# A hybrid decoder step: S5 recurrence as scans, stacked sample products, four state buffers

## The chip, the cores and the metric

The program runs on one core of a Trainium2 chip. The metric is the device time of one execution in microseconds (us), as the median of several runs. PE is the tensor engine, DVE the vector engine, ACT the scalar engine, POOL the GpSimd engine and SP the queue that issues most loads.

## The reference

One step of a two-layer trunk over a prompt of 256 tokens and eight samples of one token each (264 columns together), width 1024. A layer is

```
u = rmsnorm(x);  z = u @ w_in
S5:        h[t] = lbar * h[t-1] + bbar @ z[t]   (complex, 32 groups x 64 states), y = Re(C h) + D z, gated
retention: S = gamma * S + k^T v;  out = q S    (4 heads, 128 x 256), group norm, swish gate
conv:      causal depthwise convolution over 31 taps, layer norm, swish, projection
x = x + w_out(sum over the branches of sigmoid(gate) * projection)
x = x + FFN(rmsnorm(x))        dense in layer 0, two of eight experts in layer 1
```

The states after the step are outputs too. For each sample and head the retention state is read, decayed, the outer product of its key and value is added, and the result is written back and multiplied with the sample's query.

## The kernel before, in words

Activations lie with channels on partitions and the 264 columns along the free dimension. Weights stream through a ring of five chunks of eight 128 x 128 blocks. ACT rounds each chunk to a high part (`high_weights`, line 968, the copy at 976), DVE takes the rest as a low part (`low_weights`, line 1278, the subtraction at 1283), and PE sums three single-pass products per block (`weight_tile`, line 583, lines 577 to 579). DVE and ACT split two chunks ahead, and they do it inside their waits: each waits for a tile only after the chunks up to that tile's chunk plus two are split.

Every PE product goes to one of eight PSUM banks. The order of the tiles is written out in `tile_order` (line 72), `tile_counts` (line 132) gives each its place, a tile's bank is its place modulo eight, and PE waits in `open_tile` (line 565) until the tile that had the bank before is evicted by DVE or ACT.

The mixer of a layer, in the order of PE. The combined projection (`cb`, `ca`, `zs`, `q`, `k`, `v`); DVE turns `q` and `k` and runs convolution taps in between (`conv_ops`, lines 1366 to 1379). Then transposes: `vt` and `kt` of the prompt, `vs` and `ks` of the eight samples (ACT copies `vt`, `vs`, `ks` out, DVE `kt` at line 1441), then `win` and `kk` for S5. POOL meanwhile builds the S5 matrices of the layer (lines 1788 to 1835: powers of lbar, products with B and C); its semaphore `gb_ready` lets ACT and DVE go on behind the transposes. POOL then issues the loads of the S5 input, of the first two sample states and of the table for the S5 output.

Retention of the prompt, per head: the scores (`sc`, lines 700 and 701), multiplied with the decay by DVE, then output (`ou`, lines 712 and 714) and state (`st`, line 719). PE computes the scores of head h+1 ahead of `ou` and `st` of head h. DVE has 44 convolution taps in front of the first head and eight behind each. Then come the S5 inputs `si` (line 732), two column halves of PE in turn, and the layer norm of the convolution (`cm`, `cv`).

Then the loop over the eight samples, in which the eight tiles of the convolution's projection are spread. A turn b on PE is: gate weights `gc` (8 blocks), the output product `os` of sample b-1 (line 749: eight products in fp32, the state as stationary operand, one moving column), projection `pc` (4 blocks), outer products `oa` and `ob` (line 763: four fp32 products of 8 rows, the keys masked to sample b by DVE at line 1475). On DVE a turn is: four steps of the S5 recurrence over 32 chunks of eight tokens (`recur`, line 1381), `pc` times gate, four state updates (line 1507), the mask for sample b+2. POOL stores state b, and when PE has read it and the store has landed, loads state b+2 into the same buffer (lines 1871 to 1878); there are two buffers. ACT copies each `os` out.

Behind the loop: PE sums for the group norm (`gm`, `gv`, line 610), the S5 output `y` from the input, the table and the chunk states `hst`, then the remaining gates and projections. All products that work on q, k, v, states and S5 are fp32, which PE runs in two records each.

## Time and profile before

| | us |
|---|---|
| runs | 2072.83, 2074.55, 2078.42; median 2074.55 |
| the profiled execution | 2078.80, its span 2076.7 |
| PE busy (share of the span) | 1953.4 (94%) |
| DVE busy | 1585.2 (76%) |
| ACT busy | 1171.4 (56%) |
| POOL busy | 348.5 (17%) |
| sample loops of layers 0 and 1 | about 196 to 256 and 798 to 864 |

Busy time of PE contains overlap of neighbouring products. A timeline row gives start, duration (of the whole group when it has a count), engine, line, operation, output <- inputs, and in brackets the idle time ahead of it with the engine that ended it. A row of the chain of waits gives start, duration, engine and output.

### The profile page before, as it was taken

Reading aid. Unit: us, or ns where it says so; the run is one execution under the profiler, and the core shown is the slowest. Engines: PE = TensorE matmul, PEld = TensorE weight load, DVE = VectorE, ACT = ScalarE, POOL = GpSimd, SP = SyncE. Lnnn points to the kernel's source line nnn. Section 1 sums busy time; section 2 is a strip of 40 time slices with the busy share of each in tenths; the row PEclk is TensorE's granted clock in tenths of the full one; section 3 lists DMA queues with packets and bytes.
Section 4 is the critical chain, followed back from the end, with each engine's and each line's share of the span. In section 5 each row is a group of like instructions: output and inputs, shape, how many; then the busy total and the mean of one; then the engine's idle time right before and its main releaser. Section 6 shows DMA issues by size and latency. Waiting matters only on the chain.

```text
span 2076.7 us, 32156 instructions
## 1 busy us (share of the span) xinstructions
PE 1953.4 (94%) x12016; PEld 1657.9 (80%) x12016; DVE 1585.2 (76%) x1980; ACT 1171.4 (56%) x1209; POOL 348.5 (17%) x423
## 2 busy tenths in 40 slices
PE   7777999979998978999989999999999999999995
PEld 7766889979998977889977777777777777777774
DVE  6998855766545996746558888888888888888886
ACT  5333245444444443254456777767767776777775
POOL 7982100993000130100000000000000000000000
PEclk9989999989999997999969999999999999999998
DMA  5438625535555746535639999999999999999996
GB/s 195 143 91 137 219 75 167 184 110 183 183 173 154 213 101 137 157 112 181 242 141 355 368 383 351 387 360 365 371 370 378 354 379 364 370 371 366 382 358 233
DMA packets 98102, 527.57 MB, mean 254 GB/s; under 512 B 11864, under 2 KB 13432, under 8 KB 54360
## 3 DMA queue, kind: packets, MB, share of 16 engines
q1 hardware_dynamic: 86167, 488.69, 64.4%
q0 software_dynamic: 10784, 36.50, 8.2%
q8 instruction: 65, 1.06, 0.2%
q10 hardware_dynamic: 1056, 1.08, 0.1%
q14 instruction: 30, 0.24, 0.0%
HBM read 505.69 MB, written 20.54 MB: 253 GB/s over the span
## 4 chain that ended last, share of the span: by engine, by line
PE 78%; DVE 9%; POOL 6%; issue 3%; ACT 3%; DMA 1%; DVEq 0%; ACTq 0%; SPq 0%; POOLq 0%
PE bank L577 23%; PE bank L579 23%; PE bank L578 23%; POOL s5m L1761 3%; DVE zone L1377 3%; PE bank L763 1%; PE bank L749 1%; POOL work L1761 1%; DVE s5m_parts L1678 1%; PE bank L610 1%; PE bank L917 1%; PE bank L792 1%; PE bank L788 1%; ACT zone_parts L1229 1%; PE bank L872 1%
## 5 line engine op out<-in xcount | busy, mean ns | idle before, releaser
L1678 DVE TENSOR_TENSOR s5m_parts<-s5m,ring_parts 128x2048 fp32r<-128x2048 f32 x228 | 519.3, 2288 | 77.3 <-ACT ring_parts L1229 77.1
L1283 DVE TENSOR_TENSOR ring_parts<-ring,ring_parts 128x1024 fp32r<-128x1024 f32 x238 | 311.5, 1310 | 223.2 <-ACT ring_parts L976 221.9
L1229 ACT ACTIVATE ring_parts<-s5m 128x2048 fp32r<-128x2048 f32 x228 | 431.6, 1915 | 87.8 <-DMA s5m<-in_experts 81.7
L577 PE MATMUL bank<-uT_parts,ring_parts 128*128 128x264 f32 x1312 | 386.2, 294 | 39.4 <-DVE uT_parts L1300 21.0
L578 PE MATMUL bank<-uT_hi,ring_parts 128*128 128x264 f32 x1312 | 379.5, 289 | 0.0
L579 PE MATMUL bank<-uT_hi,ring_parts 128*128 128x264 f32 x1312 | 378.6, 289 | 0.0
L577 PE MATMUL bank<-s5m_parts,work_parts 128*112 128x512 f32 x896 | 359.1, 401 | 0.3 <-DVE table_parts L1671 0.3
L976 ACT ACTIVATE ring_parts<-ring 128x1024 fp32r<-128x1024 f32 x238 | 251.3, 1056 | 190.5 <-PE bank L579 169.0
L1678 DVE TENSOR_TENSOR s5m_parts<-s5m,zone_parts 128x2048 fp32r<-128x2048 f32 x112 | 255.9, 2288 | 67.1 <-ACT zone_parts L1229 66.9
L577 PEld LDWEIGHTS bank<-uT_parts,ring_parts 128*128 128x128 f32 x1312 | 254.4, 194 | 51.8 <-issue 45.5
L578 PEld LDWEIGHTS bank<-uT_hi,ring_parts 128*128 128x128 f32 x1312 | 255.3, 195 | 0.1
L579 PE MATMUL bank<-ring_parts,work_parts 128*112 128x512 f32 x640 | 254.1, 397 | 0.0
L579 PEld LDWEIGHTS bank<-uT_hi,ring_parts 128*128 128x128 f32 x1312 | 253.8, 193 | 0.0
L578 PE MATMUL bank<-ring_parts,table_parts 128*112 128x512 f32 x640 | 253.1, 396 | 0.0
L1229 ACT ACTIVATE zone_parts<-s5m 128x2048 fp32r<-128x2048 f32 x112 | 213.0, 1915 | 36.9 <-DMA s5m<-in_experts 35.3
L577 PEld LDWEIGHTS bank<-s5m_parts,work_parts 128*112 128x112 f32 x896 | 156.7, 175 | 49.5 <-issue 0.4
L577 PE MATMUL bank<-zone_parts,ring_parts 128*128 128x264 f32 x592 | 174.7, 295 | 8.8 <-DVE zone_parts L1300 8.8
L577 PE MATMUL bank<-s5m_parts,zone_parts 128*112 128x512 f32 x448 | 177.1, 395 | 0.0
L578 PEld LDWEIGHTS bank<-ring_parts,table_parts 128*112 128x112 f32 x640 | 113.0, 176 | 36.0
L579 PEld LDWEIGHTS bank<-ring_parts,work_parts 128*112 128x112 f32 x640 | 112.0, 175 | 37.1
L577 PEld LDWEIGHTS bank<-zone_parts,ring_parts 128*128 128x128 f32 x592 | 112.9, 191 | 10.4 <-issue 7.8
L1377 DVE SCALAR_TENSOR_TENSOR zone<-zone,vecs 128x256 f32<-128x256 f32 x240 | 117.1, 557 | 0.0
(283 smaller groups left out, 3126.5 us busy)
## 6 DMA issues: line engine op xcount, KB each, us to landing
s5m<-in_experts SPq DMA_DIRECT2D x340, 1024.0 KB, 6.7
ring<-in_weights SPq DMA_DIRECT2D x238, 512.0 KB, 3.3
work<-in_sret POOLq DMA_DIRECT2D x16, 512.0 KB, 4.7
out_ret_s<-work POOLq DMA_DIRECT2D x16, 512.0 KB, 4.8
s5m<-kscr POOLq DMA_DIRECT2D x16, 256.0 KB, 10.9
xT<-in_xT SPq DMA_DIRECT2D x1, 1056.0 KB, 5.1
zscr<-zone ACTq DMA_DIRECT2D x2, 528.0 KB, 5.8
work<-in_bc POOLq DMA_DIRECT2D x2, 512.0 KB, 4.9
```

The source lines that it names most:

```text
L577: pe.matmul(out, left[0], right[1], start=first, stop=False)
L578: pe.matmul(out, left[1], right[0], start=False, stop=False)
L579: return pe.matmul(out, left[0], right[0], start=False, stop=last)
L610: mm = pe.matmul(out[:, 0:T], ones[:, :], terms(i), start=(i == 0), stop=(i == n - 1))
L749: mm = pe.matmul(out[:, x:x + 1], sring[:, b % 2, h, half * P:(half + 1) * P], qs[:, h, b:b + 1], start=True, stop=True)
L763: mm = pe.matmul(out[:, x * DV:(x + 1) * DV], kmask[0:NS, b % 2, h * P:(h + 1) * P], vst[0:NS, h * DV:(h + 1) * DV], start=True, stop=True)
L976: act.activation(weights_hi(c), weights(c, ring), ACT.Copy).then_inc(high_done, 1)
L1229: act.activation(high_slot(c), slot(c, s5m), ACT.Copy).then_inc(high_done, 1)
L1283: dve.tensor_tensor(weights(c, ring_parts), weights(c, ring), f32(weights_hi(c)), ALU.subtract).then_inc(low_done, 1)
L1377: dve.scalar_tensor_tensor(out=cT[:, m, 0:SEQ], in0=xc[:, m, k:k + SEQ], scalar=vec(l, V_DWW, m * TAPS + k), in1=cT[:, m, 0:SEQ], op0=ALU. ...
L1678: dve.tensor_tensor(slot(c, s5m_parts), slot(c, s5m), f32(high_slot(c)), ALU.subtract).then_inc(low_done, 1)
L1761: last = pool.tensor_tensor(out[:, js], x[:, js], y[:, js], op)
```

## The change

The S5 recurrence over the prompt's chunks is taken apart: POOL computes, per state, the unit phases of lbar's eighth power for all 32 chunks by doubling (`turns`) and its magnitude (`damp`); DVE turns the inputs back by the phase, runs two real scans along the 16 x 32 columns, and turns the result forward (`sweep`, spread over turns 2 to 6 of the loop). The vs and ks tiles are stored as three stacked row groups (high, low, high and high, high, low parts at rows 0, 32 and 64), so that one single-pass product over 72 rows gives the outer product. The output product has the query as stationary operand, eight columns of which one is not zero, and the state as moving operand; head h writes rows 32h to 32h + 7 of one bank, in which all eight samples are summed; the bank is cleared by one product first, and copied, transposed and copied out once behind the loop (`ot`). Bank 7 is kept for that tile and for the norms' sums; all others rotate over seven banks. There are four state buffers; the third and fourth lie where the prompt's `vtok` was, and are loaded when `st` is done. Scores are computed right ahead of each head's output.

Cut to its core (waits and declarations that only follow from it are left out):

```diff
-o += [((l, "sc", 0), 0)]
 for h in range(HEADS):
-  if h + 1 < HEADS:
-    o += [((l, "sc", h + 1), 0)]
-  o += [((l, "ou", h), 0), ((l, "st", h), 0)]
+  o += [((l, "sc", h), 0), ((l, "ou", h), 0), ((l, "st", h), 0)]
...
+add("ot", 1)
...
-place[key] = i
+if key[1] == "os" or i > 0 and key[1] in ("ms1", "ms2"):
+  place[key] = long * NBANK + ROTATING
+  long += key[1] != "os" or key[2] == NS - 1
+else:
+  place[key] = turn // ROTATING * NBANK + turn % ROTATING
+  turn += 1
...
-l8 = sb("l8", [P, 4, GJ])
-rec = sb("rec", [P, 3, 2, GJ])
-qs = sb("qs", [P, HEADS, NS])
+qm = sb("qm", [P, HEADS, NS * NS])
+pick = sb("pick", [P, NS])
...
+os_rows = work[:, 1536:1536 + DV]
 sring = work[:, 4352:6400].rearrange("p (b h x) -> p b h x", b=2, h=HEADS)
+sring2 = zone[:, 8472:10520].rearrange("p (b h x) -> p b h x", b=2, h=HEADS)
+states = [sring[:, 0], sring[:, 1], sring2[:, 0], sring2[:, 1]]
...
+    for h in range(HEADS):
       out = open_tile((l, "sc", h))
...
            ).then_inc(mm_done, 1)
-    scores(0)
-    for h in range(HEADS):
-      if h + 1 < HEADS:
-        scores(h + 1)
       out = open_tile((l, "ou", h))
       pe.wait_ge(*out_of((l, "sc", h)))
       for half in range(2):
...
-      out = open_tile((l, "os", b))
+      if b == 0:
+        out = open_tile((l, "os", b))
+        pe.wait_ge(pick_ready, 5)
+        pe.matmul(out[:, 0:DV], ident[96:P, :], pick[96:P, :].unsqueeze(1).broadcast_to([32, DV // NS, NS]),
+             start=True, stop=False)
+      else:
+        out = at((l, "os", b))
       pe.wait_ge(*out_of((l, "oa", b)))
       pe.wait_ge(*out_of((l, "ob", b)))
-      for x in range(KD):
-        h, half = x // 2, x % 2
-        mm = pe.matmul(out[:, x:x + 1], sring[:, b % 2, h, half * P:(half + 1) * P],
-               qs[:, h, b:b + 1], start=True, stop=True)
+      for h in range(HEADS):
+        mm = pe.matmul(out[32 * h:32 * h + NS, 0:DV], qm[:, h, b * NS:(b + 1) * NS], states[b % 4][:, h, :],
+               start=False, stop=(b == NS - 1))
       mm.then_inc(mm_done, 1)
...
     for b in range(NS):
...
-          mm = pe.matmul(out[:, x * DV:(x + 1) * DV], kmask[0:NS, b % 2, h * P:(h + 1) * P],
-                 vst[0:NS, h * DV:(h + 1) * DV], start=True, stop=True)
+          mm = pe.matmul(out[:, x * DV:(x + 1) * DV], kmask_parts[0:STACK, b % 2, h * P:(h + 1) * P],
+                 vst_parts[0:STACK, h * DV:(h + 1) * DV], start=True, stop=True)
...
     sample_output(NS - 1)
+    out = open_tile((l, "ot", 0))
+    pe.wait_ge(*out_of((l, "os", NS - 1)))
+    for half in range(2):
+      mm = pe.transpose(out[:, half * P:(half + 1) * P], os_rows[:, half * P:(half + 1) * P], ident[:, :])
+    mm.then_inc(mm_done, 1)
...
+      key = (l, "vs", i)
+      full(key)
+      if i == 0:
+        act.wait_ge(stack_zero, l + 1)
+      for lo in (64, 0):
+        last = act.activation(vst_parts[lo:lo + NS, i * 512:(i + 1) * 512], at(key)[0:NS, :], ACT.Copy)
+      last.then_inc(stack_high, 1)
+    key = (l, "ks", 0)
+    full(key)
+    for lo in (32, 0):
+      last = act.activation(kst_parts[lo:lo + NS, :], at(key)[0:NS, :], ACT.Copy)
+    last.then_inc(stack_high, 1)
...
-      if d > 0:
-        sample_out(d - 1)
-    sample_out(NS - 1)
+    key = (l, "os", NS - 1)
+    copy_out(key, os_rows, at(key)[:, 0:DV])
+    key = (l, "ot", 0)
+    full(key)
+    for half in range(2):
+      last = act.activation(vT[:, half:KD:2, SEQ:T],
+                 at(key)[:, half * P:(half + 1) * P].rearrange("p (h x) -> p h x", h=HEADS)[:, :, 0:NS],
+                 ACT.Copy)
+    last.then_inc(freed(key), 1)
...
+  def squared(to_re, to_im, re, im):
+    link(mul(W(14), W(re), W(re)))
+    link(mul(W(15), W(im), W(im)))
+    link(dve.tensor_tensor(W(to_re), W(14), W(15), ALU.subtract))
+    return dve.scalar_tensor_tensor(out=W(to_im), in0=W(re), scalar=2.0, in1=W(im), op0=ALU.mult, op1=ALU.mult)
...
+  dve.wait_ge(lam_ready, 2)
+  link(squared(4, 5, 7, 6))
+  link(squared(10, 11, 4, 5))
+  link(squared(4, 5, 10, 11))
+  link(mul(W(14), W(4), W(4)))
+  link(mul(W(15), W(5), W(5)))
+  link(add(W(14), W(14), W(15)))
+  link(dve.tensor_scalar(W(14), W(14), -0.5, 1.5, ALU.mult, ALU.add))
+  mul(W(4), W(4), W(14)).then_inc(phase_ready, 1)
+  link(mul(W(5), W(5), W(14)))
+  link(mul(W(14), W(3), W(3)))
+  link(mul(W(14), W(14), W(14)))
+  mul(W(1), W(14), W(14)).then_inc(phase_ready, 1)
...
+  dve.memset(qm[:, :, :], 0.0).then_inc(pick_ready, 1)
+  dve.memset(pick[:, :], 0.0).then_inc(pick_ready, 1)
+  dve.wait_ge(pick_ready, 2)
+  for lo in (0, 32, 64):
+    dve.tensor_copy(pick[lo:lo + NS, :], ident[0:NS, 0:NS]).then_inc(pick_ready, 1)
...
                     op0=ALU.mult, op1=ALU.add).then_inc(conv_step, 1)
...
-      link(add(hst[:, :, :, to], rec[:, 1, :, :], rec[:, 2, :, :]))
+  def sweep(l, d):
+    re, im = (turns[:, r] for r in range(2))
+    both = re.unsqueeze(1).broadcast_to([P, 2, GJ, NC])
+    if d == 2:
+      dve.wait_ge(turns_ready, l + 1)
+      for i in range(4):
+        evicted_by_act((l, "si", i))
+      mul(driven, si[:, :, :, 0:NC], both).then_inc(dve_order, 1)
+      mul(swept[:, 0], si[:, 1, :, 0:NC], im).then_inc(dve_order, 1)
+      order[0] += 2
+      link(mul(swept[:, 1], si[:, 0, :, 0:NC], im))
+    elif d == 3:
+      link(add(driven[:, 0], driven[:, 0], swept[:, 0]))
+      link(dve.tensor_tensor(driven[:, 1], driven[:, 1], swept[:, 1], ALU.subtract))
+      link(dve.tensor_tensor_scan(swept[:, 0].rearrange("p j t -> p (j t)"), damp,
+                    driven[:, 0].rearrange("p j t -> p (j t)"), 0.0, ALU.mult, ALU.add))
+    elif d == 4:
+      link(dve.tensor_tensor_scan(swept[:, 1].rearrange("p j t -> p (j t)"), damp,
+                    driven[:, 1].rearrange("p j t -> p (j t)"), 0.0, ALU.mult, ALU.add))
+      link(mul(driven, swept, both))
+    elif d == 5:
+      mul(cross, swept[:, 1], im).then_inc(dve_order, 1)
+      order[0] += 1
+      link(mul(damp.rearrange("p (j t) -> p j t", j=GJ), swept[:, 0], im))
+    elif d == 6:
+      if l > 0:
+        dve.wait_ge(hstate_out, 32 * l)
+      for r, op, part in ((0, ALU.subtract, cross), (1, ALU.add, damp.rearrange("p (j t) -> p j t", j=GJ))):
+        dve.tensor_tensor(hst[:, r, :, 1:NC], driven[:, r, :, 0:NC - 1], part[:, :, 0:NC - 1], op)
+        dve.tensor_tensor(hfin[:, r, :], driven[:, r, :, NC - 1], part[:, :, NC - 1], op)
...
-    dve.tensor_copy(qs[:, :, :], qT[:, :, SEQ:T]).then_inc(qs_ready, 1)
+    dve.tensor_copy(qm[:, :, 0:NS * NS:NS + 1], qT[:, :, SEQ:T]).then_inc(qs_ready, 1)
...
+    for i in range(2):
+      c = slice(i * 512, (i + 1) * 512)
+      key = (l, "vs", i)
+      dve.wait_ge(stack_high, 3 * l + i + 1)
+      dve.tensor_tensor(vst_parts[32:32 + NS, c], at(key)[0:NS, :], f32(vst_parts[0:NS, c]), ALU.subtract
+               ).then_inc(freed(key), 1)
+    key = (l, "ks", 0)
+    dve.wait_ge(stack_high, 3 * l + 3)
+    dve.tensor_tensor(kst_parts[64:64 + NS, :], at(key)[0:NS, :], f32(kst_parts[0:NS, :]), ALU.subtract
+             ).then_inc(freed(key), 1)
     conv_ops(l, 48, 92)
...
-      dve.tensor_scalar(kmask[0:NS, b % 2, :], kst[0:NS, :], ident[0:NS, b:b + 1], None, ALU.mult
+      dve.tensor_scalar(kmask_parts[0:STACK, b % 2, :], f32(kst_parts[0:STACK, :]), pick[0:STACK, b:b + 1], None, ALU.mult
...
     link(dve.memset(hst[:, :, :, 0:1], 0.0))
     for d in range(KD):
-      recur(l, 4 * d, 4 * d + 4)
+      sweep(l, d)
...
-          s = sring[:, d % 2, h, :]
+          s = states[d % 4][:, h, :]
...
-    if l > 0:
-      dve.wait_ge(hstate_out, 32 * l)
-    link(dve.tensor_copy(hfin[:, :, :], hst[:, :, :, NC + NS]))
...
-    for w, r in ((0, 0), (1, 0), (3, 1)):
-      link(pool.tensor_copy(l8[:, w, :], pa[:, r, S, :]))
-    pool.tensor_scalar(l8[:, 2, :], pa[:, 1, S, :], -1.0, 0.0, ALU.mult, ALU.add).then_inc(l8_ready, 1)
...
+    link(pool.memset(f32(kst_parts[0:STACK, :]), 0.0))
+    pool.memset(f32(vst_parts[0:STACK, :]), 0.0).then_inc(stack_zero, 1)
     mul(dd, ident[0:GP, 0:GP].unsqueeze(1).broadcast_to(few), dskip[:, l, :].unsqueeze(2).broadcast_to(few)
       ).then_inc(gb_ready, 1)
...
       pool.wait_ge(*out_of((l, "st", h)))
+    for b in range(2, 4):
+      pool.dma_start(states[b], a["sret"][l, b].rearrange("h d v -> d h v")).then_inc(s_in[b], 16)
     pool.dma_start(a["ret_p"][l].rearrange("h d v -> d h v"), stst[:, :, :]).then_inc(st_out, 16)
...
+    pool.wait_ge(phase_ready, 2)
+    pool.wait_ge(mm_done, DONE[(l, "si", 3)])
+    for r in range(2):
+      link(pool.tensor_copy(turns[:, r, :, 0], lw[:, 4 + r, ls]))
+    link(pool.tensor_copy(damp.rearrange("p (j t) -> p j t", j=GJ), lw[:, 1, ls].unsqueeze(2).broadcast_to([P, GJ, NC])))
+    link(pool.memset(damp.rearrange("p (j t) -> p j t", j=GJ)[:, :, 0:1], 0.0))
+    n = 1
+    while n < NC:
+      product([turns[:, r, :, n:2 * n] for r in range(2)], [turns[:, r, :, 0:n] for r in range(2)],
+          [turns[:, r, :, n - 1:n].broadcast_to([P, GJ, n]) for r in range(2)], cross[:, :, 0:n])
+      n *= 2
+    pool.tensor_copy(cross[:, 0:1, 0:1], damp[:, 0:1].unsqueeze(2)).then_inc(turns_ready, 1)
...
-      if b + 2 < NS:
...
+      if b + 4 < NS:
...
         pool.wait_ge(mm_done, DONE[(l, "os", b)])
-        pool.wait_ge(s_out[b % 2], 16 * (4 * l + b // 2 + 1))
-        pool.dma_start(sring[:, b % 2, :, :], a["sret"][l, b + 2].rearrange("h d v -> d h v")).then_inc(s_in[b % 2], 16)
+        pool.wait_ge(s_out[b % 4], 16 * (2 * l + b // 4 + 1))
+        pool.dma_start(states[b % 4], a["sret"][l, b + 4].rearrange("h d v -> d h v")).then_inc(s_in[b % 4], 16)
...
```

## Rows read from the trace of the kernel before

**Rows 1.** Stretches: us; busy PE, PEld, DVE, ACT, POOL; PE clock, DMA share, GB/s.
```profile
200.00:255.00 55.00, 54.90 (x396) 50.23 (x396) 46.33 (x190) 12.82 (x22) 9.80 (x13) 1.00 0.72 226
...
804.00:818.00 14.00, 14.00 (x71) 12.54 (x71) 10.16 (x46) 1.63 (x3) 2.26 (x3) 0.63 0.52 174
```

**Rows 2.** Timeline of DVE, end of the constants' operations (start, duration).
```profile
13.10 0.19 DVE L1303 TENSOR_TENSOR lw<-lw 128x32 f32<-128x32 f32 x1
```

**Rows 3.** Groups by line on DVE, 55 to 131 us: busy us, mean ns.
```profile
L1377 DVE SCALAR_TENSOR_TENSOR zone<-zone,vecs 128x256 f32<-128x256 f32 x37 | 32.9, 944 | 0.0
L1283 DVE TENSOR_TENSOR ring_parts<-ring,ring_parts 128x1024 fp32r<-128x1024 f32 x17 | 29.0, 1704 | 0.0
```

**Rows 4.** Timeline of POOL, layer 0: fills, copies, two-input operations.
```profile
5.44 1.41 POOL L1776 MEMSET s5m<- 128x1536 f32 x1
...
28.79 1.76 POOL L1809 COPY l<-work 128x16 f32<-128x16 f32 x3
...
30.82 1.32 POOL L1746 TENSOR_TENSOR work<-lw,work 128x256 f32<-128x256 f32 x2
```

**Rows 5.** Timeline of DVE, the long run of taps, layers 0 and 1.
```profile
138.05 1.29 DVE L1441 TENSOR_TENSOR work<-bank,kdec 128x512 f32<-128x512 f32 x2 [0.94 <-POOL work L1746]
139.26 17.51 DVE L1377 SCALAR_TENSOR_TENSOR zone<-zone,vecs 128x256 f32<-128x256 f32 x44
...
738.76 17.50 DVE L1377 SCALAR_TENSOR_TENSOR zone<-zone,vecs 128x256 f32<-128x256 f32 x44
```

**Rows 6.** Timeline of ACT, copies of the transposed tiles, both layers.
```profile
138.05 2.07 ACT L994 ACTIVATE zone<-bank 128x512 f32<-128x512 f32 x4 [7.40 <-POOL work L1746]
139.98 1.53 ACT L994 ACTIVATE work<-bank 8x512 f32<-8x512 f32 x3
...
734.16 2.71 ACT L994 ACTIVATE zone<-bank 128x264 f32<-128x264 f32 x5 [1.56 <-PE bank L579]
```

**Rows 7.** Timeline of PE (layers 0, 1) and DVE (layer 0) at the scores.
```profile
161.16 0.59 PE L700 MATMUL bank<-zone 128*128 128x256 f32 x2
...
761.27 0.60 PE L700 MATMUL bank<-zone 128*128 128x256 f32 x2
...
157.21 3.72 DVE L1377 SCALAR_TENSOR_TENSOR zone<-zone,vecs 128x256 f32<-128x256 f32 x8
```

**Rows 8.** Timeline of DVE ahead of the loop, layer 0.
```profile
190.92 1.47 DVE L1300 TENSOR_TENSOR zone_parts<-zone,sq_parts 128x264 fp32r<-128x264 f32 x4 [2.48 <-ACT sq_parts L990]
```

**Rows 9.** The sample loops: PE timeline, groups from 200 to 255, chain of waits.
```profile
200.04 1.92 PE L749 MATMUL bank<-qs,work 128*128 128x1 f32 x16 [0.47 <-DVE work L1507]
...
208.39 1.84 PE L749 MATMUL bank<-qs,work 128*128 128x1 f32 x16
...
L1283 DVE TENSOR_TENSOR ring_parts<-ring,ring_parts 128x1024 fp32r<-128x1024 f32 x10 | 12.3, 1226 | 1.8 <-ACT ring_parts L976 1.6
L1507 DVE SCALAR_TENSOR_TENSOR work<-work,bank 128x256 f32<-128x256 f32 x27 | 10.1, 416 | 2.0 <-PE bank L763 1.9
...
252.78 0.12 PE bank L578
253.02 1.93 PE bank L763 x8
...
255.87 3.42 PE bank L749 x16
...
259.75 3.56 PE bank L610 x8
...
803.49 1.92 PE bank L749 x16
...
864.03 3.56 PE bank L749 x16
```

**Rows 10.** Timeline of PE, S5 input products, layer 0.
```profile
171.34 3.94 PE L732 MATMUL bank<-s5m 128*64 128x48 f32 x128
```

**Rows 11.** DMA issues: size, median us to landing.
```profile
out_ret_p<-zone POOLq DMA_DIRECT2D x2, 512.0 KB, 24.7
```

81 lines of the change are left out of this document (39 added, 42 removed).

## The prediction

> **What bounds the kernel now.** I read the page first, for the slices in which TensorE (PE) is not full, then the table of stretches, then the chain of waits, then the timeline engine by engine where that chain leaves PE. The change touches only the mixer of each of the two layers, about 0 to 300 us and 650 to 900 us, so what matters is what ends last there. In the loop over the eight samples PE is busy for 54.9 of 55 us in layer 0 at a granted clock of 1.00, while VectorE (DVE) is busy for 46.3 [rows 1]: the loop is bound by PE, and its round, from one sample's output product to the next, is 208.39 - 200.04 = 8.35 us in its first turn [rows 9]. In front of the loop it is different: there the chain of waits runs through GpSimd (POOL) and DVE, and what is added on DVE, or between ScalarE (ACT) and DVE, is paid in full. One more reading carries weight: while POOL computes, DVE's operations with two inputs in SBUF are slow. A tap of the convolution takes 944 ns beside POOL and 17.51 / 44 = 398 ns without it, the split of a weight chunk 1704 against 1226 ns [rows 3, 5, 9].
>
> **The change, part by part.**
>
> *Ahead of the first norm (layer 0).* DVE gets 21 small linked operations and five small fills and copies. The row of their kind takes 0.19 us [rows 2], 0.23 with the hand-over to the next; so 21 x 0.23 = 4.8, plus 0.7 for the fills: 5.5 us. DVE goes straight on from there, so the first split activations are late by that much. Little of it shows at once: at 138.05 DVE waited 0.94 us for POOL's matrices anyway [rows 5], and what is left, 4.6 us, now runs after POOL is done, at 398 in place of 944 ns a tap: about 2.2 us.
>
> *POOL's building of the S5 matrices.* The four copies of the eighth power go: 1.76 us for three, 2.0 with the fourth. Two fills of 512 and 1024 columns come, 1536 columns as in the row of 1.41 us [rows 4]. POOL is done 0.6 us earlier, in layer 0 alone on the chain.
>
> *Stacked rows.* ACT copies each small transposed tile twice, and DVE subtracts, before the long run of 44 taps. In layer 0 ACT needs 2.07 us for its four large copies from POOL's end at 137.4, then six small ones at 1.53 / 3 = 0.51 [rows 6]: 142.5. DVE's last subtraction, some 0.65 as one of the two in the row of 1.29 [rows 5], ends at 143.2; the taps began at 139.26. That is +3.9 us, which contains the 2.2 above, as the two delays overlap. In layer 1 ACT's large copies end at 734.16 + 2.71 = 736.9, the six at 740.0, DVE at 740.7 against 738.76 [rows 5, 6]: +1.9 us.
>
> *Scores back in their place.* Now PE multiplies the scores of the next head only behind this head's output and state, and DVE asks for them after eight taps (3.72 us at the first head). In layer 0 a score product that stands behind the first head's output and state starts at 161.16; with its own 0.65 and a hand-over, DVE has it at 162.0, and was ready at 157.21 + 3.72 = 160.9: +1.1, and 0.4 for later heads. In layer 1 it is 761.27 + 0.9 = 762.2 against 738.76 + 17.50 + 0.6 + 3.7 = 760.5: +1.7, and 0.2 for later heads [rows 5, 7]. The upper bound is a PE as slow at every head as at the first, where output and state take 161.16 - 157.3 = 3.9 us: with 1.3 for the scores and the hand-over 5.4 against 3.8 on DVE, +1.6 four times, 6.4 us a layer. The lower is zero, at full clock. I take 1.5 and 1.9.
>
> *The tables for the scans, on POOL.* Some 34 operations, none but one larger than the 256 elements of the row of 0.66 [rows 4]: under 34 x 0.7 = 24 us with the gaps, from the last S5 input product (171.34 + 3.94 + 5 = 180.3 [rows 10]) to 204 at the latest. DVE asks for them in its third round, at about 211, so the wait itself costs nothing; if they come later, every us costs one, as PE's weights queue behind DVE. But in that stretch DVE normalises the convolution. Its two-input operations there, one of 1056 elements, four splits (1.47 us [rows 8]) and two weight chunks, are some 5.2 us; at 1704 / 1226 they cost 2.0 us more, per layer. Between nothing and twice that.
>
> *The first round.* Four steps of the recurrence (3.2 us) go from in front of DVE's first chunks, but then ACT's second chunk is what is late: I give back 1.0 us. So the first sample's output product starts at +6.4 in layer 0 (3.9 + 1.5 + 2.0 - 1.0) and +4.8 in layer 1 (1.9 + 1.9 + 2.0 - 1.0).
>
> *A round of the loop on PE.* The outer products took 1.93 us; in one pass they are four products of 256 columns at 0.12 each (the pace of the weight products of 264 columns), 0.6 with the entry. The output product was 16 loads of weights, 1.8 us [rows 9]. It is now four products with 8 columns of weights and 256 moving columns, two passes of 0.215 us each as the score row has it (0.43 from 161.16 for two [rows 7]): 1.7 us if they run one after the other. That the four go to different columns of the array may let them overlap. The row for that are the S5 input products, 64 columns wide and alternating: 128 records in 3.94 us, 31 ns each [rows 10], where 48 moving columns at that pace take 40. Overlap there is partial. I take one pass of each overlapping the next product, 5 x 0.215 = 1.1 us. With 24 weight products for the gate (3.0 us with the entry) and 12 for the projection (1.6), a round is 3.0 + 1.6 + 0.6 + 1.1 = 6.3 us; 6.9 if nothing overlaps.
>
> The Trainium skill, TensorEngine Tiling (Array Packing), section Tiling Modes, says that tiles run independently and in parallel; by that the output product is 0.5 us and the round 5.7. The same section says that a change of tiling mode drains the engine, which speaks against this change with two such changes a round; the row of such tiles at 171.34 shows no idle time in front of it [rows 10], so this trace does not show that price.
>
> *A round on DVE.* Four updates at 0.416, 1.5 weight chunks at 1.23 [rows 9], product and mask 0.9: 4.4 us, and the scan part on top, priced as two-input operations at 1.23 for 1024 elements: 2.5 us in the third round, 1.3 plus a scan in the fourth, a scan plus 1.2 in the fifth, under 1.8 later. No row shows a scan. At the pace of a two-input operation its 512 elements take 0.6; as each element needs the one before, it may be three times that, 1.8. I take the nearest row's 0.6: 6.9, 6.3 and 6.2 us in these rounds, and with PE's 6.3 in the others and something for hand-overs a mean round of 6.5. The high end adds 2 us a layer. The Trainium skill, DVE: opcode table, instruction layouts, handler registers and perf-mode slots, in its paragraph on feedback, has the scan at half throughput; by that it takes 1.1, and the loop is 1 us longer a layer.
>
> *States.* Loads for samples 2 and 3 join POOL's queue in front of the prompt's state, behind the tables of the S5 output; the transfer that stood there took 24.7 us to land [rows 11]. Issued at about 178, they land by 206, wanted at about 213: hidden, with 7 us to spare. On POOL the first store now stands behind the tables, to 204 at the latest, and is due at about 205. Four buffers leave the later loads three rounds; nothing waits.
>
> *From first to last output product:* six rounds of 6.5 and a last one without the gate's product (1.1 + 1.6 + 0.6, and 1.6 for DVE): 43.9 us. Before it was 255.87 - 200.04 = 55.8 and 864.03 - 803.49 = 60.5 [rows 9]. Layer 1's loop lost some 5 us at a clock of 0.63 [rows 1]; I let half of that come back. Saved: 11.9 and 14.0.
>
> *Tail.* Between the last output product and the group norm's sums lay 3.88 us [rows 9]; now the product at the lower clock 2.1, copy 0.6, two transposes 0.8, copies 0.6, hand-overs: 4.5, +0.6. DVE's part behind the loop is off the path.
>
> *Sum.* Layer 0: 6.4 - 11.9 + 0.6 = -4.9. Layer 1: 4.8 - 14.0 + 0.6 = -8.6. Together -13.5 us, against the profiled execution's 2078.8 (span 2076.7 and 2.1 around it). That execution is 4.2 above the median of 2074.55, so in terms of the median: 2061. Seven banks in rotation in place of eight cost nothing that I find: each tile's bank is freed well before, with one tile more of distance gone; if that cover goes, ACT's small copies in front of the taps are where it would show.
>
> **Rivals.** *The output products run side by side.* Then PE's round is 5.7 and DVE's 4.4 to 6.9 decides more of them; mean 6.0, 0.5 less in 12 rounds: 2055. For: PE does overlap records [rows 10]. Against: only partly.
>
> *The front eats the gain.* PE stays as slow through the scores as at the first head and DVE waits at each: 6.4 in place of 1.5 and 1.9, and the normalisation pays POOL twice the 2.0: 13.4 us more, 2074, no change. For: PE is idle for long before the scores, and slow at the first head. Against: its score product of the second head is over in 0.59 us, half of what the low clock would need [rows 7].
>
> *The loop falls to the lower clock: slower.* With PE's 6.3 us doubled a round takes 12.6 and costs 6.1 us more than the 6.5 of the sum. So 2.2 slow rounds of the twelve in both layers eat the 13.5 us; with four it is 2061 + 24 = 2085. For: layer 1 had 14 us at a clock of 0.63 before, with PE busy all along [rows 1], and a PE that waits for DVE in the rounds of the scans is less busy than before. Against: layer 0 stayed at 1.00.
>
> **How the numbers follow.** The forecast has 0.50, the side-by-side case 0.15, the eaten front 0.23, the slow loop 0.12. The range, 2047 to 2076, runs from the side-by-side case with the front 4 us a layer cheaper to just past the eaten front; it leaves out the slow loop and some of the edges. About 0.3% (6.2 us) is what a measurement can tell. Faster than 2068.3: nearly all of the first two and some of the third, 0.69; slower than 2080.8: 0.12; the rest, 0.19.
>
> **What would show it.** Right: the loop's round near 6.5 us, PE no longer full in the third to fifth; the first tap 2 to 4 us later against the matrices; DVE waiting about 1 to 2 us for the second head's scores; the tables done before the third round. Wrong: a round over 7, DVE waiting for tables or a state, a granted clock well under 1 in the loop, or a front more than 10 us later.

## The result, and the profile after

Faster by far more than forecast: 2040.62 us, the median of four runs (2037.32 to 2043.15), against 2073.69, the median of four of the kernel before; the ratio is 0.9833, with a 95% interval of 0.9817 to 0.985. That is 33 us, where the prediction had 13.5 and a range that ended at 2047. The profiled execution took 2041.88 us, its span 2039.9, at a mean granted clock of 0.966 (0.96 before).

PE is busy for 1903.0 us (1953.4 before), DVE for 1566.1 (1585.2). To see where the time went, I cut both spans at three products that both kernels have: the first sums of the group norm in each layer, and DVE's first use of the prompt's keys in layer 1. From the start to the group norm of layer 0: 259.75 us before, 247.34 after, -12.4. From there to the keys of layer 1, which the change leaves alone: 477.8 and 475.9, -1.9. To the group norm of layer 1: 130.5 and 113.0, -17.5. From there to the end, left alone too: 1208.7 and 1203.7, -5.0. The two stretches that the change does not touch make up 6.9 of the 36.8 us between these two executions; that they vary from one execution to the next is the subject of one of the runs below. Of the 33 us some 27 to 30 lie in the two mixers, by the one or the other execution of the kernel before.

The loops, as the table of stretches shows them (us; busy PE, PEld, DVE, ACT, POOL; PE clock, DMA share, GB/s), where [rows 1] had PE full and a clock of 1.00 and 0.63:

```profile
206.00:246.00 40.00, 36.95 (x320) 32.35 (x312) 35.41 (x68) 11.72 (x16) 7.99 (x12) 1.00 0.81 286
795.00:834.00 39.00, 36.17 (x312) 32.34 (x312) 35.27 (x66) 11.55 (x15) 8.08 (x11) 1.00 0.80 269
```

PE and DVE are now about equally full, 92 and 89%. In the timeline of PE (start, duration), L765 is the output product, L781 the outer products, L788 the transposes behind the loop, L627 the group norm's sums; the first product of layer 0, the round behind it, the one product that waits inside the loop, the last two and the end of that loop, and the first and last of layer 1:

```profile
205.86 0.62 PE L765 MATMUL bank<-work,qm 128*8 128x256 f32 x8
207.97 0.63 PE L781 MATMUL bank<-work_parts 72*128 72x256 f32 x4
211.45 0.62 PE L765 MATMUL bank<-work,qm 128*8 128x256 f32 x8
...
229.68 0.62 PE L765 MATMUL bank<-work,qm 128*8 128x256 f32 x8 [1.15 <-DVE work L1596]
...
240.87 0.62 PE L765 MATMUL bank<-zone,qm 128*8 128x256 f32 x8
...
245.15 0.62 PE L765 MATMUL bank<-zone,qm 128*8 128x256 f32 x8 [1.53 <-DVE zone L1596]
246.36 0.41 PE L788 MATMUL bank<-ident,work 128*128 128x128 f32 x2 [0.59 <-ACT work L1016]
247.34 5.49 PE L627 MATMUL bank<-zone,ones 128*128 128x264 f32 x16 [0.57 <-ACT zone L1123]
...
794.50 0.62 PE L765 MATMUL bank<-work,qm 128*8 128x256 f32 x8
...
833.80 0.62 PE L765 MATMUL bank<-zone,qm 128*8 128x256 f32 x8 [1.54 <-DVE zone L1596]
```

The first round is 211.45 - 205.86 = 5.59 us (8.35 in [rows 9]). The rounds are 5.59 to 5.79 us but for one in each loop, 6.84 us, in which PE waits 1.15 us for DVE's update of the state; the mean of the six full rounds is (240.87 - 205.86) / 6 = 5.84 us (forecast 6.5). From the first to the last output product lie 39.3 us in both layers (55.8 and 60.5 in [rows 9]; forecast 43.9). The eight records of an output product take 0.62 us together.

The front of layer 0 on DVE, to be held against [rows 5]: the keys, the subtractions for the stacked rows, the taps, the first two heads' scores, then the splits ahead of the loop ([rows 8] had 1.47):

```profile
139.79 1.27 DVE L1522 TENSOR_TENSOR work<-bank,kdec 128x512 f32<-128x512 f32 x2
...
144.16 0.68 DVE L1533 TENSOR_TENSOR work_parts<-bank,work_parts 8x512 fp32r<-8x512 f32 x1 [0.53 <-ACT work_parts L1080]
144.87 17.51 DVE L1439 SCALAR_TENSOR_TENSOR zone<-zone,vecs 128x256 f32<-128x256 f32 x44
162.30 0.61 DVE L1339 TENSOR_TENSOR work<-bank,table 128x256 f32<-128x256 f32 x2
...
167.56 0.62 DVE L1339 TENSOR_TENSOR work<-bank,table 128x256 f32<-128x256 f32 x2 [1.02 <-PE bank L717]
...
197.16 2.52 DVE L1336 TENSOR_TENSOR zone_parts<-zone,sq_parts 128x264 fp32r<-128x264 f32 x4 [2.48 <-ACT sq_parts L1012]
```

The keys are 1.7 us later than before, the taps 5.6, the first output product 5.8. The last of these varies: with the same front, the profiles of the runs below have that product at 205.5 to 209.1. And the scans, with the weight chunks they stand beside (groups on DVE from 206 to 246 us: busy us, mean ns):

```profile
L1319 DVE TENSOR_TENSOR ring_parts<-ring,ring_parts 128x1024 fp32r<-128x1024 f32 x10 | 12.0, 1223 | 1.0 <-ACT ring_parts L998 0.9
L1596 DVE SCALAR_TENSOR_TENSOR zone<-zone,bank 128x256 f32<-128x256 f32 x16 | 5.6, 414 | 0.0
L1458 DVE TENSOR_TENSOR_SCAN s5m<-s5m 128x512 f32<-128x512 f32 x1 | 1.2, 1225 | 0.0
```

### The profile page after: what moved, and what is told of

It is laid out like the page before. It is cut to its first block, busy times and chain, and to the rows that moved or that the text cites. A ratio compares the mean times of both kernels' runs of the same rounds, so it can differ in the third digit from the quotient of the medians.

```text
span 2039.9 us, 31590 instructions
## 1 busy us (share of the span) xinstructions
PE 1903.0 (93%) x11832; PEld 1607.3 (79%) x11832; DVE 1566.1 (77%) x1718; ACT 1171.5 (57%) x1205; POOL 381.9 (19%) x489
## 4 chain that ended last, share of the span: by engine, by line
PE 77%; DVE 9%; POOL 6%; issue 4%; ACT 3%; DMA 1%; DVEq 0%; ACTq 0%; SPq 0%; POOLq 0%
PE bank L594 23%; PE bank L596 23%; PE bank L595 23%; POOL s5m L1847 3%; DVE zone L1439 2%; POOL work L1847 1%; PE bank L627 1%; DVE s5m_parts L1764 1%; PE bank L939 1%; PE bank L814 1%; PE bank L810 1%; DVE ring_parts L1319 1%; ACT zone_parts L1265 1%; PE bank L894 1%; DVE s5m L1339 1%
## 5 line engine op out<-in xcount | busy, mean ns | idle before, releaser
L594 PEld LDWEIGHTS bank<-zone_parts,ring_parts 128*128 128x128 f32 x592 | 112.1, 189 | 16.4 <-issue 13.5
L1277 ACT ACTIVATE s5m<-bank 112x512 f32<-112x512 f32 x56 | 33.5, 598 | 146.4 <-PE bank L596 146.3
## 6 DMA issues: line engine op xcount, KB each, us to landing
zone<-in_sret POOLq DMA_DIRECT2D x8, 512.0 KB, 13.8
```

What stands on the lines that cost most here:

```text
L594: pe.matmul(out, left[0], right[1], start=first, stop=False)
L1277: act.activation(hm[0:CAP, t % 2, :], bank[t % 2][0:CAP, :], ACT.Silu).then_inc(evicted[t % 2], 1)
```

## The experiments

Each run is given as its ratio to the kernel before on the same chip, with the 95% interval; the changed kernel itself has 0.9833 (0.9817 to 0.985), and 0.9847 (0.9824 to 0.987) when it was run once more beside three of the others. An interval reaches 2 to 5 us to either side, so small differences are read from the traces. The edits are cut to their core.

> The changed kernel once more, beside the next three: 2038 to 2043 us.

It took 2043.65 us (median of six), where 2038 to 2043 was expected.

**What makes the round shorter than forecast: the output products.** All four on one group of columns:

```diff
+row = 32 * h if b == NS - 1 else 0
-mm = pe.matmul(out[32 * h:32 * h + NS, 0:DV], qm[...], states[b % 4][:, h, :],
+mm = pe.matmul(out[row:row + NS, 0:DV], qm[...], states[b % 4][:, h, :],
```

> The changed kernel with the four output products of a sample written to one and the same group of eight columns of the array instead of four groups (the last sample of a layer keeps its four). The samples' outputs of the heads are so added up; nothing else is left out. Theory A (the four products run side by side on four column groups, and PE's round of 5.6 us is that of the loop): one product group goes from 0.62 to some 8 x 0.215 = 1.7 us, 1.1 us more in each of seven rounds, less the 1 to 2 us that PE idles in a loop now: 6 to 8 us a layer, 2053 to 2056 us. Theory B (they overlap little, as the prediction took it, and the short loop has another cause): 0 to 2 us a layer, 2041 to 2045 us.

2058.87 us, ratio 0.9929 (0.9913 to 0.9946): 18 us slower than the changed kernel. Its timeline of PE:

```profile
207.82 1.89 PE L766 MATMUL bank<-work,qm 128*8 128x256 f32 x8
211.21 0.64 PE L782 MATMUL bank<-work_parts 72*128 72x256 f32 x4
214.69 1.89 PE L766 MATMUL bank<-work,qm 128*8 128x256 f32 x8
```

The same eight records take 1.89 us on one group of columns and 0.62 on four, and the round grows by the difference of 1.27, from 5.59 to 6.87 (214.69 - 207.82). Theory A holds, a little over its upper end: the products run side by side, three times as fast on four groups as on one, and PE sets the round. The two layers' loops are 14.9 us longer together (46.76 us each); the other 3 us are within the intervals (in the two profiles 1.8).

**Whether the scans decide any round.** The sweep taken out of DVE's rounds:

```diff
-sweep(l, d)
...
+dve.memset(hst[:, :, :, 1:NC], 0.0)
+link(dve.memset(hfin[:, :, :], 0.0))
```

> The changed kernel without the scans' part on DVE in the rounds (the states of the S5 recurrence stay zero; tables and all else as they were). Theory A (PE alone sets the loop of the changed kernel, and DVE's scans fit beside it): the round stays at 5.6 us and 0 to 2 us a layer come off: 2037 to 2041 us. Theory B (DVE decides the rounds with scans, as the prediction's sum of 6.2 to 6.9 us for them had it): 3 to 4 us a layer, 2033 to 2035 us.

2043.17 us, ratio 0.9847 (0.9831 to 0.9863): no change. In its timeline the full rounds are all 5.59 us, as here:

```profile
214.68 0.62 PE L765 MATMUL bank<-work,qm 128*8 128x256 f32 x8
220.27 0.62 PE L765 MATMUL bank<-zone,qm 128*8 128x256 f32 x8
```

The loop is 37.8 us, 1.5 less than with the scans: the one round of 6.84 us is gone. So the scans' operations, some 10 us of DVE's time in a loop, cost 1.5: theory A. That the time does not show 3 us for two layers is within the intervals; in the profile the first output product comes at 209.09, 3.2 us later than in the changed kernel, and the edit changes nothing ahead of it.

**What each half is worth without the other.** First the 32 steps of the recurrence in place of the scans, with the new products:

```diff
-sweep(l, d)
+recur(l, 4 * d, 4 * d + 4)
...
-product([turns[:, r, :, n:2 * n] for r in range(2)], ...)
+link(mul(l8[:, 0, :], lw[:, 1, ls], lw[:, 4, ls]))
...
```

> The changed kernel with the 32 steps of the recurrence, four a round, in place of the scans and of the tables for them; all products as in the changed kernel. Theory A (PE and DVE are in balance in the new loop, 5.6 us a round each, so each half of the change is worth its time only with the other): DVE's round is 4.15 + 4 x 0.8 = 7.35 us, the loop 7 x 1.75 = 12.3 us longer and the first round 3 us later, 26 to 31 us for two layers: 2066 to 2072 us, nearly the kernel before. Theory B (PE alone sets the round, as in the kernel before): only the first round, 2 to 3 us a layer, 2045 to 2047 us.

2060.65 us, ratio 0.9927 (0.9901 to 0.9953). PE now waits for DVE in every round:

```profile
212.10 0.62 PE L767 MATMUL bank<-work,qm 128*8 128x256 f32 x8 [0.75 <-DVE work L1614]
...
219.63 0.62 PE L767 MATMUL bank<-zone,qm 128*8 128x256 f32 x8 [1.16 <-DVE zone L1614]
...
226.04 0.62 PE L767 MATMUL bank<-zone,qm 128*8 128x256 f32 x8 [0.75 <-DVE zone L1614]
```

The rounds are 7.53 and 6.41 us in turn, with two weight chunks to split and with one. The loop is 47.8 us. A's mechanism is right; its size was at least 5 us too large: the mean round is 6.97 us and not 7.35, and the first round was no later (205.69).

Then the scans with both old products (the two edits that follow, together):

> The changed kernel with both old forms of the products: outer products in fp32 on eight rows without stacked rows, states as weights in the output products; scans, tables, four buffers and the place of the scores stay. Theory A (with the old products PE's round is 8.35 us, as before, and faster DVE work hides behind it): the loop is as long as before, and the time is that of the kernel before with the front 0 to 4 us later: 2072 to 2078 us. Theory B (the scans bring their share by themselves): 2058 to 2063 us.

2075.51 us, ratio 1.0003 (0.9993 to 1.0014): theory A, no gain at all. Its loop in layer 0 is 55.76 us from 205.88 to 261.64, that of the kernel before 55.83:

```profile
214.15 1.84 PE L762 MATMUL bank<-qm,work 128*128 128x1 f32 x16
...
222.40 1.84 PE L762 MATMUL bank<-qm,zone 128*128 128x1 f32 x16
```

So the scans alone give 0, the products alone 13 us (10 to 20 by the interval), both 33, each with the four buffers and the new front: with the old products PE's round of 8.25 us hides what DVE does, steps or scans; with the new ones DVE's steps become the bound, and only then are the scans worth their 20 us.

**The two products by themselves.** The output products with the states as weights:

```diff
-mm = pe.matmul(out[32 * h:32 * h + NS, 0:DV], qm[:, h, b * NS:(b + 1) * NS], states[b % 4][:, h, :], ...)
+mm = pe.matmul(out[:, NS * x + b:NS * x + b + 1], states[b % 4][:, h, half * P:(half + 1) * P],
+               qm[:, h, b * (NS + 1):b * (NS + 1) + 1], start=True, stop=True)
```

> The changed kernel with the output products of the kernel before: sixteen loads of states as weights with one moving column, each sample's in columns of its own of the one bank, one copy at the end, no transposes. Theory A: PE's round is 5.6 - 0.55 + 1.85 = 6.9 us, 9 us more in seven rounds less 1 to 2 us of idle PE, and about 1 us at the tail: 8 to 10 us a layer, 2057 to 2061 us. Theory B (the products were worth 0.7 us a round as the prediction had it, and DVE decides the scan rounds): 2 to 4 us a layer, 2045 to 2049 us.

2050.97 us, ratio 0.9888 (0.9868 to 0.9908). The round is 6.63 us, 1.04 more, and the loop 45.2 us (5.9 more). Between the two theories: the row of the old product shows 1.84 us, but it takes only 6.63 - 5.04 = 1.59 of the round (5.04 is 5.59 less the 0.55 after which the next product starts behind the new one).

The outer products on eight rows in fp32:

```diff
-kmask_parts[0:STACK, b % 2, h * P:(h + 1) * P], vst_parts[0:STACK, h * DV:(h + 1) * DV]
+kmask[0:NS, b % 2, h * P:(h + 1) * P], vst[0:NS, h * DV:(h + 1) * DV]
```

> The changed kernel with the outer products on eight rows in fp32, and so without the stacked rows: ACT copies each small tile once, DVE subtracts nothing, POOL fills nothing. Theory A: PE's round is 5.6 - 0.47 + 1.93 = 7.06 us, 10 us more in seven rounds less 1 to 2 of idle PE, and the front 3 us (layer 0) and 2 us (layer 1) shorter: 5 to 6 us a layer, 2050 to 2053 us. Theory B (the stacked rows cost the front nothing that shows): 8 to 10 us a layer, 2057 to 2061 us.

2062.84 us, ratio 0.9941 (0.9923 to 0.996), 22 us more than the changed kernel and outside both theories. The rounds are 7.22 us, as A had them within 0.2, but two of layer 0 are 8.77, at a granted clock of 0.81 in place of 1.00; the loops are 12.2 and 9.2 us longer. By rounds, the outer products are worth 7.22 - 5.59 = 1.63 us and the output products 1.04, together what lies between 8.25 and 5.59. The front is shorter too: the sums of the convolution start at 180.54 in place of 183.91. But the first outer products, ahead of the loop, run at the lower clock there (3.78 us, 1.99 inside the loop):

```profile
197.15 3.78 PE L781 MATMUL bank<-work 8*128 8x256 f32 x8
...
205.92 0.62 PE L765 MATMUL bank<-work,qm 128*8 128x256 f32 x8
```

They end at 200.9, where the changed kernel's, 1.06 us long, end at 201.4, and the first output product starts at 205.92 against 205.86. In this execution, what the stacked rows cost in front of the taps they give back ahead of the loop; theory A had counted the first alone.

**The four buffers.**

```diff
-states = [sring[:, 0], sring[:, 1], sring2[:, 0], sring2[:, 1]]
+states = [sring[:, 0], sring[:, 1]]
```

> The changed kernel with two buffers for the samples' states instead of four. Theory A (a buffer needs its store, 6.8 us, and its load, 6.9, and the issue behind them, more than two rounds of 5.6 us): DVE waits for states, a round is 7 to 7.5 us, 8 to 11 us a layer less 2 us where PE stands in layer 1: 2055 to 2062 us. Theory B (two rounds hide it, as before): 2038 to 2043 us.

2066.29 us, ratio 0.9961 (0.9947 to 0.9975), even more than A's upper end. The waits of DVE in the loop of layer 0 (us in total, times, longest):

```profile
DVE work L1594 <- DMA work<-in_sret: 9.8, 6, 5.1
```

In the changed kernel no such wait is in the trace. In the profiles the two loops are 10.9 and 7.3 us longer. The buffers are not a detail: without them some 25 of the 33 us are gone.

**The costs at the front, taken out one by one.** Scores one head ahead:

```diff
+scores(0)
 for h in range(HEADS):
+  if h + 1 < HEADS:
+    scores(h + 1)
-  out = open_tile((l, "sc", h))
```

> The changed kernel with each head's scores multiplied one head ahead again, as in the kernel before. Theory A (the place of the scores costs what the prediction gave, 1.5 and 1.9 us, seen as 1.4 and 2.3): 3 to 4 us less than the changed kernel, 2036 to 2038 us. Theory B (in layer 1 the convolution's sums wait for something else, the 4.5 us in which PE stands in the middle of the S5 input products): layer 0 alone, 1 to 1.5 us less, 2039 to 2040 us.

2036.32 us, ratio 0.9812 (0.9788 to 0.9836). DVE's wait is gone (second head at 166.66 behind 162.49, 4.2 us; 5.3 in the changed kernel), and the convolution's sums start 1.3 us earlier in layer 0 (182.64 against 183.91) and 3.5 in layer 1 (767.16 against 770.67, of which 0.7 were there at the keys). Theory A by the trace, with a caution: with the scores not ahead, that wait of DVE was 1.0 us in the changed kernel, but 2.1 to 2.4 us in four other profiles with the same scores and stacked rows, at a granted clock of 0.70 to 0.80 from 165 to 172 us (0.93 in the changed kernel). Beside the changed kernel on the same chip the time is 7.3 us less (2036.32 against 2043.65); the intervals overlap.

Stacked rows later:

```diff
 # ACT, in place of the copies to the stacked rows
+copy_out((l, "vs", i), kmask[0:NS, i, :], at((l, "vs", i))[0:NS, :])
...
 # DVE, behind conv_done
+dve.tensor_tensor(vst_parts[32:32 + NS, c], kmask[0:NS, i, :], f32(vst_parts[0:NS, c]), ALU.subtract)
```

> The changed kernel with the stacked rows built later: ACT copies each small tile once into free rows, makes the high parts between the heads' scores, DVE subtracts behind the convolution, POOL fills behind its matrices. Theory A (the stacking in front of the taps is paid in full): the taps start 3 to 4 us earlier in layer 0 and 2 us in layer 1, and 4 to 6 us come off: 2035 to 2037 us. Theory B (the subtractions then stand in front of the convolution's sums and take it back, or something else is late there): 0 to 2 us, 2039 to 2041 us.

2037.71 us, ratio 0.9808 (0.9784 to 0.9833). That is 5.9 us less than the changed kernel beside it on that chip, and the intervals just overlap. In layer 0 the taps start 3.9 us earlier, but of that 1.4 go to a longer wait for the second head's scores, and the loop's end is 0.9 us earlier:

```profile
139.79 1.27 DVE L1525 TENSOR_TENSOR work<-bank,kdec 128x512 f32<-128x512 f32 x2
140.99 17.49 DVE L1442 SCALAR_TENSOR_TENSOR zone<-zone,vecs 128x256 f32<-128x256 f32 x44
...
165.09 0.62 DVE L1342 TENSOR_TENSOR work<-bank,table 128x256 f32<-128x256 f32 x2 [2.44 <-PE bank L718]
```

By its time it lies between the theories. This cost and that of the scores may stand behind one another, so that each alone shows only a part; but a wait of that length for the second head's scores is also in profiles where the stacked rows are not late, so that is not shown by this run.

The phases on POOL:

```diff
 # POOL, layer 0, ahead of the wait for kk
+product([W(i) for i in to], x, x, W(14))   (three squarings, then the norm)
```

> The changed kernel with the 21 small operations for the scans' phases on POOL, where it waits for the S5 matrices, instead of on DVE ahead of the first norm. Theory A (of the 5.6 us only the 1.7 show that are left where DVE first needs POOL): 1.5 to 2 us less, 2038.5 to 2039.5 us. Theory B (all of it shows in the end): 5 to 6 us less, 2035 to 2036 us.

2040.78 us, ratio 0.9837 (0.9813 to 0.9861), which tells it from the changed kernel (0.9847 on that chip) no better than chance. By its trace the start of layer 0 gains nothing. The first half of the keys is 1.6 us earlier, as A had it, but the second waits for PE (139.98), and the taps start at 144.61 against 144.87: ACT's copies for the stacked rows end at nearly the same time and are what DVE waits for.

All three together:

> The changed kernel with the three edits to the front together: scores one head ahead, stacked rows built later, the phases' operations on POOL. Theory A (the three stand one behind the other on the chain, so their gains add): the loop starts 6 to 7 us earlier in layer 0 and 4 us in layer 1, 9 to 11 us come off: 2030 to 2033 us. Theory B (behind the first of them the chain goes over POOL's matrices or the S5 input products, which none of them moves): 5 to 6 us, 2035 to 2037 us.

2042.43 us, ratio 0.9852 (0.9835 to 0.9868): nothing is gained, which neither theory had. The loop of layer 0 does start earlier, at 198.00 in place of 205.86, but it takes 51.5 us in place of 39.3. POOL's operations for the phases now stand in front of everything else on its queue, from 144.49 to 167.05 (timeline of POOL, start and duration). The largest wait in the loop is for weights, and behind it stand those for what POOL delivers (waits of ACT and DVE, 190 to 252 us; then PE's timeline):

```profile
144.49 12.18 POOL L1820 TENSOR_TENSOR lw<-lw 128x32 f32<-128x32 f32 x2
...
204.88 0.19 POOL L1968 COPY s5m<-s5m 128x1 f32<-128x1 f32 x1
```

```profile
ACT ring_parts L1006 <- DMA ring<-in_weights: 18.2, 3, 13.2
...
DVE ring_parts L1330 <- ACT ring_parts L1006: 6.7, 4, 3.4
DVE zone L1584 <- DMA zone<-in_sret: 3.1, 2, 1.7
...
DVE s5m L1350 <- POOL s5m L1968: 2.3, 1, 2.3
DVE work L1584 <- DMA work<-in_sret: 1.9, 1, 1.9
```

```profile
212.19 0.59 PE L597 MATMUL bank<-uT_parts,ring_parts 128*128 128x264 f32 x1 [4.40 <-DVE ring_parts L1330]
```

A weight chunk that was asked for at 188.0 landed 21.8 us later. PE stood 4.4 us for it and did the rest of that round at a clock of 0.50, so that this round alone took 13.3 us in place of 5.6. POOL had issued the loads of the S5 input, the states and the store of the prompt's state from 175.5 to 184.5 us; in the run below, which differs in POOL's operations alone, they go out from 164.8 to 175.9, and no such wait is in its loop. That the late transfers hold the weights up is an inference from these times.

That left two readings, a front that is worth nothing or a front whose gain went to POOL's queue. So the first two edits without the third:

> The changed kernel with two of the three edits to the front: scores one head ahead and stacked rows built later, the phases' operations where the changed kernel has them, so that POOL's tables and the states' transfers are not late. Theory A (the two costs of the front are real and add once POOL is not in the way; with the third edit the gain at the front was lost to POOL's queue): the loop starts 5 us earlier in layer 0 and 4 in layer 1, 6 to 9 us less than the changed kernel: 2032 to 2036 us. Theory B (the front's gain is lost whatever POOL does): 2039 to 2043 us.

2030.05 us, ratio 0.9789 (0.9768 to 0.981): 10 us less than the changed kernel, under A's range, and the fastest of all. Its loops are 39.3 us again, and start at 202.26 and 780.28:

```profile
202.26 0.62 PE L775 MATMUL bank<-work,qm 128*8 128x256 f32 x8
207.85 0.62 PE L775 MATMUL bank<-work,qm 128*8 128x256 f32 x8
...
752.48 4.01 PE L753 MATMUL bank<-s5m 128*64 128x48 f32 x128
...
780.28 0.62 PE L775 MATMUL bank<-work,qm 128*8 128x256 f32 x8
```

So POOL's operations are what took the gain, some 12 us between the two runs. Layer 0 gains 3.6 us and the mixer of layer 1 10.4 (from its keys at 719.19 to its group norm at 821.78, 102.6 us against 113.0). Some 2.5 of the latter belong to a stretch in which PE stood still in the changed kernel (last section) and which is missing here: there the convolution's sums start at 770.67, 4.0 us behind the end of its last operation on DVE, 766.65; elsewhere that takes 1.5. That stretch is also missing in two runs whose edits lie behind it, so those 2.5 us are hardly the edits'.

**How much of the difference is the kernel before's one execution.**

> The kernel before once more, for its profile: the loop of layer 1 from the first output product to the last, 60.5 us in the profile shown, against 55.8 in layer 0. Theory A (the 5 us at a granted clock of 0.63 belong to this kernel, whose PE comes out of a long idle stretch in layer 1): again 59 to 61 us. Theory B (they belong to that one execution): 55.8 to 57 us, and then some 4 us of what the changed kernel gains in layer 1 by the two profiles is not of the change.

Its time was 2071.71 us, span 2069.6. The loop of layer 1 took 57.35 us (804.63 to 861.98), between the theories and nearer to B (57.3 too in the run with the scans alone, which has the same products):

```profile
804.00:818.00 14.00, 13.83 (x93) 12.74 (x92) 11.70 (x52) 3.31 (x7) 3.02 (x4) 0.88 0.67 226
```

The same stretch had a granted clock of 0.63 in [rows 1]. Cut at the same products, this execution has 261.23, 477.3, 125.9 and 1205.2 us. Against it the changed kernel gains 13.9 and 12.9 us in the two layers' mixers and 1.4 and 1.6 elsewhere. In layer 0 its loop is as long as before (55.8 us) but starts 2.9 us later:

```profile
202.90 1.84 PE L749 MATMUL bank<-qs,work 128*128 128x1 f32 x16
```

The granted clock from 192 to 200 us was 0.50 there, 0.84 in the execution of [rows 9], with the same products and no wait that differs. So what the change costs ahead of a loop is known to some 3 us only.

## Why the prediction was wrong

The direction was right, and so was the reading of the bound: PE's products set the loop, and the front is on the chain. The gain was forecast 2.4 times too small. The step that failed is the round of the loop on PE, where the overlap of the output products was taken too small; the rule for DVE's part of the rounds comes next. By the prediction's own steps:

- **Ahead of the first norm.** 5.5 us forecast, 5.6 measured (DVE's first split at 18.82, 13.21 before). At the keys 1.7 were left; the 2.2 of the prediction was near.
- **POOL.** Its last operation for the matrices ended 0.4 us later, not 0.6 earlier: the fills took 0.52 and 0.95 us as forecast, and the copies gave 2.1 us at first (35.02 against 37.14 where they had stood), but of that 1.2 were left 100 us on, beside DVE. A miss of 1 us.
- **Stacked rows.** Forecast +3.9 and +1.9 at the first tap; measured +5.6 and, against the keys of layer 1, +2.5. ACT's copies took 0.60 us each, not 0.51, and the small ones started 1 us later than forecast, behind POOL (140.5).
- **Scores.** Forecast +1.5 and +1.9; measured +1.4 and +2.2 from the first head's scores to the last (13.0 and 13.8 us, 11.6 before). Right for this execution; the wait of layer 0, 1.0 us here, was up to 2.4 in others.
- **Tables and normalisation.** POOL was done with the tables at 199.4, and nothing waited for them. The contention was forecast at 2.0 us a layer and was 1.1 (splits 2.52 against 1.47, the multiplication 1.33 against 1.26) and 0.6.
- **First output product.** Forecast +6.4 and +4.8, measured +5.8 in layer 0 and +5.3 in layer 1 (from the keys: 71.3 us, 65.9 before). As a sum near, but by the other execution of the kernel before it is +3.0 and +5.1.
- **The round: the step that failed.** "I take one pass of each overlapping the next product, 5 x 0.215 = 1.1 us", and "a mean round of 6.5". The output product costs 0.55 us of the round, the outer products 0.47 (from 207.97 to 208.44, where the next product starts) in place of 0.6, and the round is 5.59. The nearest row was [rows 10], 31 ns a record for products of 48 columns on two alternating groups, where 40 would be without overlap. I carried that partial overlap over and did not ask what four groups give for 256 columns; no row told it, and the run on one group settles it: 0.62 us in place of 1.89. The Trainium skill, TensorEngine Tiling (Array Packing), section Tiling Modes, had it right: by its rule the round was 5.7, and 5.59 was measured. The price for a change of tiling mode that it names there is small here, if it is there at all: the output product starts 0.21 us behind the weight product ahead of it (211.24 to 211.45), the old form 0.13 (212.09 to 212.22 in the run with states as weights); what the 0.08 us are is not shown.
- **DVE in the scan rounds.** The other error in the 6.5: I added for each round the slower of the two engines, 6.9, 6.3 and 6.2 us for the scan rounds. DVE's rounds were forecast well: from one state update to the next it took 6.79, 5.90 and 6.85 us. But PE and DVE are coupled by two slots of the key mask, two of the gates, four states and seven banks, so that most of a long round of DVE is made good in a short one: PE's rounds were 5.60, 5.79 and 6.84, and it waited 1.15 us in the last of them. DVE's mean is 35.41 / 40 of the time, and without the scans the loop is just 1.5 us shorter. That the scan itself was priced at half (0.6 us forecast, 1.23 measured for 512 elements) made no difference for the same reason. The Trainium skill, DVE: opcode table, instruction layouts, handler registers and perf-mode slots, has the scan at half throughput in its paragraph on feedback, which agrees: 1024 elements of a two-input operation take 1.22.
- **Tail.** +0.6 forecast; -1.7 measured in layer 0 (2.19 us from the last output product to the group norm, 3.88 before; 2.56 in the other execution of the kernel before, which makes it -0.4). The last product ran at the full clock, 0.62 us in place of the 2.1 that I took.
- **Layer 1's low clock.** I let half of the 5 us come back. All of it is missing in the changed kernel's loop, but 3.2 of it is missing in another execution of the kernel before too, so it was hardly the change's.

The sum for layer 0: 39.3 in place of 43.9 is 4.6, the tail 2.3, the front 0.6, together 7.5 us; -4.9 forecast, -12.4 measured. By the other execution of the kernel before it is 4.6, 1.0 and 3.4, and -13.9 measured: the loop is the part that stands in both. Of its 4.6 us, PE's round at 5.6 in place of 6.3, under the rule of the slower engine (6.9, 6.3, 6.2 and three of 5.6), and the allowance for hand-overs make 2.8, that rule 1.2, the last round 0.6. In layer 1 it was -8.6 forecast against -17.5 by the two profiles shown and -12.9 by the other execution, with the same errors.

The rival with the output products side by side named the cause, and gave it 0.15. Its 2055 was still too high. Its mean round of 6.0 explains some 2 us of that; the rest lies in the tails, the front, layer 1's clock and the stretches that the change leaves alone. The other two rivals did not come about: DVE waited once a layer for scores, and the granted clock in the loop was 1.00. The eaten front was also added up too high: it has four waits for scores a layer, and there are three.

## What to carry to other kernels

Products with few columns that go to different column groups ran side by side here (0.62 us on four groups, 1.89 on one): count the records of one group, not of all. Where two engines hand work back and forth through several slots, compare their mean work over the loop before the slower of each round, and look where the slots run out; and when one engine is cut, look whether the other is cut as well, since a cut of either alone may be worth nothing. An edit that moves work to an idle engine has to be followed down that engine's queue: here it took a gain of 10 us back. And before a small difference at the front is put down to an edit, look how much the same front differs between executions: 3 us here.

## What the hardware showed that I had not expected

POOL can be shut out for the whole of a run of DVE operations. In the changed kernel one two-input operation of 16 x 512 elements on POOL took 8.96 us, and ended 1.1 us behind DVE's 44 taps (144.87 + 17.51 = 162.38); with the phases on POOL the same operation took 1.30 us beside the same taps:

```profile
154.53 8.96 POOL L1934 TENSOR_TENSOR s5m<-s5m,work 16x512 f32<-16x512 f32 x1 [8.18 <-ACT s5m L1016]
```

```profile
156.78 1.30 POOL L1926 TENSOR_TENSOR s5m<-s5m,work 16x512 f32<-16x512 f32 x1
```

With all three front edits two operations of 128 x 32 elements took from 144.49 to 156.67, again until just behind the taps (138.76 + 17.50 = 156.26); such a pair takes 0.71 us later. When POOL gets in between two taps and when not, these runs do not settle.

PE stood still for 4.5 us in the middle of the S5 input products of layer 1, with nothing in the profile that it waited for, while the DMA engines were full (stretch 764 to 769 us, DMA share 1.20):

```profile
768.79 1.95 PE L743 MATMUL bank<-s5m 128*64 128x48 f32 x32 [4.52 <-issue]
```

It was 4.7 us in the changed kernel's other profile, 3.9 with the scores ahead, 1.8 with the stacked rows late, and absent with both. But it was also absent with the output products on one group and with the states as weights, whose edits lie behind it, so its length is not put down to the front's edits. In the two profiles of the kernel before 2.6 and 2.9 us stand a little later, in the convolution's sums. What PE waits for there was not tried.
